# Where the high parts of the weights lie in the second projection

## What is computed

```
p = rmsnorm(x, ln_g[l]) @ w_in[l]          # 1024 -> 3584 columns: the projection
mixer a, b, c = p[:2304] ; xq = next 256 ; gate = last 1024
o = band attention (layer 0) or a gated linear recurrence (layer 1) on a, b, c
y = concat(o, cross_attention(xq, memory)) * silu(gate)
x = x + y @ w_out[l]
```

## The kernel before

| | place before |
|---|---|
| x, high and low parts, 9 slots (`x.slot`) | byte 480 of 512; slots 0 to 6 at 480 of 1024, 7 and 8 at 992 |
| one slice k of x | 1280 bytes in the first pass, 1024 later |
| weights, high part, low part and sum | byte 32 of 512, which `pj1_shift0` and `pj1_shift1` (64 bytes each) give |
| one slice k of the weights | 512 bytes |

## Time and profile before

### The profile page before, as it was taken

One profiled execution on the slowest core, in us unless ns is written; L12 is line 12 of the kernel. 1 busy time (PEld: TensorE's weight loads), 2 busy tenths in 40 slices (PEclk: granted clock), 3 DMA queues, 4 the chain that ended last, 5 costly groups with the idle time before them and its releaser, 6 DMA issues. The chain is left out here.

```text
span 2376.1 us, 61711 instructions
## 1 busy us (share of the span) xinstructions
PE 2312.2 (97%) x23787; PEld 2094.7 (88%) x23787; DVE 1819.5 (77%) x3555; ACT 1413.5 (59%) x3281; POOL 381.0 (16%) x585
## 2 busy tenths in 40 slices
PE   7999999999989999999999999999999989999998
PEld 4999999999967888888887999999999978888886
DVE  7889788887666656666666998797888777888885
ACT  4564666755565555555554564776757566666664
POOL 2332000000022221211112332000000112112111
PEclk9999999999999999999999999999999999999999
DMA  6886887769894222222226897886879793444442
GB/s 227 298 299 219 301 281 231 247 220 332 232 307 121 83 66 89 90 69 83 73 81 232 272 303 242 256 275 214 266 248 312 230 269 117 129 131 122 137 135 70
DMA packets 396664, 469.64 MB, mean 198 GB/s; under 512 B 39860, under 2 KB 248556, under 8 KB 396376
## 3 DMA queue, kind: packets, MB, share of 16 engines
q1 hardware_dynamic: 379832, 406.02, 54.4%
q0 software_dynamic: 14704, 54.92, 6.6%
q10 hardware_dynamic: 1840, 4.75, 0.7%
HBM read 318.77 MB, written 151.56 MB: 198 GB/s over the span
## 5 line engine op out<-in xcount | busy, mean ns | idle before, releaser
L1468 PE MATMUL pj_acc<-x_lo,pj_wh 128*128 128x256 f32 (+1 forms) x3080 | 780.9, 284 | 0.0
L1468 PE MATMUL pj_acc<-x_hi,pj_wh 128*128 128x256 f32 (+1 forms) x3080 | 780.8, 284 | 0.0
L1468 PEld LDWEIGHTS pj_acc<-x_hi,pj_wh 128*128 128x128 f32 x3080 | 578.4, 188 | 0.0
L1468 PEld LDWEIGHTS pj_acc<-x_lo,pj_wh 128*128 128x128 f32 x3080 | 578.4, 188 | 0.0
L509 ACT ACTIVATE pj_wh<-pj_wt 128x512 fp32r<-128x512 f32 x676 | 420.3, 634 | 255.9 <-DMA pj_wt<-tsum 175.1
L516 DVE SCALAR_TENSOR_TENSOR pj_wl<-pj_wt,pj_wh 128x512 fp32r<-128x512 f32 x676 | 467.0, 708 | 87.0 <-ACT pj_wh L509 79.3
L1464 PE MATMUL pj_acc<-x_hi,pj_wl 128*128 128x256 f32 (+1 forms) x3080 | 509.4, 287 | 13.8 <-DVE pj_wl L516 11.9
L1464 PEld LDWEIGHTS pj_acc<-x_hi,pj_wl 128*128 128x128 f32 x3080 | 425.3, 188 | 22.1 <-DVE pj_wl L516 19.5
L1307 DVE TENSOR_TENSOR pj_out<-pj_out,pj_acc 128x512 f32<-128x512 f32 (+1 forms) x448 | 320.8, 716 | 103.3 <-PE pj_acc L1468 69.7
L2541 DVE COPY pb_pt<-pb_SCTP 128x256 f32<-128x256 f32 (+2 forms) x266 | 115.8, 435 | 147.5 <-PE pb_SCTP L2352 74.3
L2676 ACT ACTIVATE pb_se<-pb_se,pb_mn 128x640 f32<-128x640 f32 (+4 forms) x208 | 154.6, 745 | 114.6 <-DVE pb_mn L2524 114.3
(11 more groups left out here) (371 smaller groups left out, 3992.1 us busy)
## 6 DMA issues: line engine op xcount, KB each, us to landing
pj_wt<-tsum SPq DMA_DIRECT2D x546, 256.0 KB, 3.8
proj<-pj_out SPq DMA_DIRECT2D x112, 512.0 KB, 4.2
tsum<-pj_wt SPq DMA_DIRECT2D x140, 256.0 KB, 3.2
pj_wraw<-in_w_in_dram POOLq DMA_DIRECT2D x24, 1024.0 KB, 6.6
tsum<-pj_wraw SPq DMA_DIRECT2D x56, 256.0 KB, 4.2
hg_x<-x_mid SPq DMA_DIRECT2D x17, 512.0 KB, 3.7
pb_gate<-proj SPq DMA_DIRECT2D x16, 512.0 KB, 5.1
pb_x<-in_x_prompt_dram SPq DMA_DIRECT2D x16, 512.0 KB, 3.8
```

Source lines behind the costliest of these rows:

```text
L1468: ins = nc.tensor.matmul(BANK[j][:, 0:n], w.hi[j][:, k], x.of(y, p, j)[:, k], start=False, stop=(k == 3 and i == 1))
```

## The change

In the second projection the high parts get buffers of 4 slices of 136 columns, of which 128 are used, so that slices lie 544 bytes apart. Ahead of term j stands an empty buffer of 128 x (j mod 4) bytes, and behind it one that fills up, so that the low part and the next term begin at byte 32 of a 512-byte period again. The high parts of the terms start at byte 32, 160, 288, 416, 32, 160 and 288 of 512. An empty buffer `pj1_pad1` is shortened so that the x slots behind term 0 stay where they were. The first projection keeps its layout.

```diff
     def term(self, j, sb, shadowed):
         l = self.l
-        self.hi[j] = sb(f"pj{l}_wh{j}", [P, 4, P], F32R)
+        if l:
+            if j % 4:
+                sb(f"pj{l}_apart{j}", [P, j % 4 * 32])
+            self.hi[j] = sb(f"pj{l}_wh{j}", [P, 4, P + 8], F32R)[:, :, 0:P]
+            if j % 4 < 3:
+                sb(f"pj{l}_again{j}", [P, 96 - j % 4 * 32])
+        else:
+            self.hi[j] = sb(f"pj{l}_wh{j}", [P, 4, P], F32R)
         with ExitStack() as shadow:
             self.sum[j] = shadowed(shadow)(f"pj{l}_wt{j}", [P, 4, P])
         self.lo[j] = sb(f"pj{l}_wl{j}", [P, 4, P], F32R)
...
                         w.term(0, sb1, sb_in)
-                        sb1("pj1_pad1", [P, 496])
+                        sb1("pj1_pad1", [P, 368])
                         for i in (1, 2, 0, 4, 5, 6):
```

## The result

| | before | after |
|---|---|---|
| median of the runs, us | 2383.94 (5 runs) | 2395.55 (5 runs) |
| ratio | | 1.0047, 95% interval 1.0035 to 1.0059 |
| span of the profiled execution, us | 2376.1 | 2392.0 |
| first rounded narrow step starts, us | 1473.97 | 1476.68 |
| last narrow step starts, us | 1886.12 | 1901.54 |

The account below looks back on a forecast made before the run. TensorE was taken to bound the second projection through the distance between matmul starts. All terms (high-part matmuls, rounding, subtraction, buffer shift) were 0, leaving the 2384.9 us median, predicted as 2385 us; range 2370 to 2398.

Parts of the forecast that it names:

- the slower rival: Second projection's high-part matmuls: changing distances lose the fast rhythm again and again; +12.7 us, 2397.6 us; chance 0.26.
- sign of being wrong: Second projection's matmul starts: a pattern by slice or term, or TensorE waiting for VectorE in the wide pass.
- What bounds the kernel: Second projection: TensorE, by distance between matmul starts, 113.3 ns in narrow passes and 146.7 ns in the wide one.
- I take 0, for four reasons: Second projection's high-part matmuls: no change, 0 us, between bounds of -24.5 and +12.7 us.
- Reasons two and three: Second projection: no slice dearer in the wide pass despite 256-byte jumps; no x slot much dearer in narrow passes.
- Reason one: Narrow passes: 117.5 and 113.3 ns rhythms have the same address distances, so addresses did not set the rhythm.
- Reason four: Attention stage's output matmuls: buffers differing by 32 bytes gave 0.22 and 0.23 us between starts, under 5%.
- The faster rival: Second projection's high-part matmuls: spread placements avoid part of the read collisions; -12.3 us, 2372.6 us; chance 0.29.
- The 8.8 us around the span: Whole kernel: median 2384.9 us against the profile's 2376.1 us; the difference was taken to lie around the span and left.
- The rounding and subtraction in four runs: Second projection: ScalarE writes and VectorE reads high parts as four runs of 128; 0 us each, subtraction at worst +2.2.

## Why the prediction was right in its range and wrong in its likeliest case

The time, 2395.55 us, lies in the range of 2370 to 2398, near the slower rival's 2397.6. The forecast itself, no change and 2385 us, was wrong: what came true is the rival that had a chance of 0.26. The range held because it had been drawn to reach that rival. The prediction's own sign of being wrong, a pattern by slice or by term in the starts, is there: in the last pass terms 0 to 6 take 1.43, 1.41, 1.42, 1.40, 1.42, 1.42 and 1.42 us a step.

- **What bounds the kernel** was right: TensorE waited even less in the narrow passes, and of the 15.8 us that their matmuls lost from start to start, 12.7 reached the end.
- **The slower rival's total** is near the time partly by luck, since its terms missed both ways. It had 9.9 us for the narrow high-part matmuls, which lost 11.1. It had nothing for the low parts' matmuls, which lost 4.7, since four at the good distance are about what the rhythm takes to come back. The shorter pauses, 3.0 us, stood nowhere in it. And it had 2.8 us for the wide pass, whose matmuls lost nothing.
- **The step that failed is "I take 0, for four reasons".** Reasons two and three looked at distances that jump by 256 and 512 bytes. Both are multiples of 128, and the runs show that just those jumps are free (offsets by term, spacing of 640). Distances of 0, 32 or 96 modulo 128 were nowhere in this stage's trace, and I read their absence as harmlessness. What the runs showed in place of the 0 is 118.4 ns for 113.7 on the matmuls with high parts.
- **Reason one** was true and its conclusion was not. Two rhythms on one layout do exist, but at distance 64 modulo 128 alone; at the others nothing below 116.8 ns lasts. That a state can change by itself doesn't show that the layout has no part in it.
- **Reason four** had the only fine distance in the trace, 32 bytes, in matmuls of 512 columns in groups of three with other instructions between. Their starts lie 226 to 240 ns apart, with medians of 231 to 233 ns on every full tile. And the two distances compared there, 0 and 96 modulo 128, are both such as never had the fast rhythm in the projection, so they could not have shown one being lost.
- **The slower rival's mechanism** was nearly the one at work: a fast rhythm that holds at one distance and is lost at slices. It was argued as a matter of change from slice to slice, and its counter-argument (the wide pass has changing distances and stays regular) rested on the same blind spot. What decides is each distance's remainder, not that it changes: 96 or 128 held constant is as slow.
- **The faster rival** (half the excess goes when meetings are spread) did not occur in any layout tried. The 109.2 ns that the prediction worked out from the Trainium skill was reached in no steady stretch of any layout, and 113.3 was the lowest. The page "TensorE: Matmul & The Clock Gate" of the Trainium skill, section "Back-to-back issue gap", gives that formula for a single matmul by itself and not for a stream with a weight load each, which the prediction didn't say.
- **The 8.8 us around the span** were a misreading: about 1.8 us lie around it in every run of the changed kernel, and the rest, by these figures, was a profiled execution quicker than the median. It did not touch the forecast, which left them as they were.
- The rounding and subtraction in four runs cost nothing, as said.

The prediction set aside a rule of the Trainium skill, page "TensorE: Matmul & The Clock Gate", section "Step-by-step: what each phase is for", that a load of the next weights takes nothing from the running matmul. It would have made this change free. For fp32r streams of 256 columns the runs speak against it: with instructions, counts and sizes equal, a distance of 96 or 128 bytes instead of 64 between the two operands' places costs 5.4 ns a matmul (118.7 against 113.3), and with both operands moved together by 64 bytes 113.3 is still reached. The page "SBUF — State Buffer", section "SBUF: two separate sides", says that TensorE never waits on anyone else's accesses. No run here contradicts that: what was moved are TensorE's own two operands. Why the distance matters, and whether a load meets the stream of its own matmul or of the one before, these runs don't tell.

## What to carry to other kernels

Where matmuls with a weight load each run without a wait, read the distance from start to start and compare it over layouts: one matmul's recorded duration hides it. Here it paid to keep every spacing of slices of either operand at a multiple of 128 bytes, so that the distance between the two has one remainder modulo 128, and to choose the good remainder, 64; for other forms the good one has to be measured. And when a trace is used to call a parameter harmless, check first that the trace holds values of the kind that the change brings in.

## What the hardware showed that was not expected

- The fast rhythm, 113.3 ns a matmul of 256 fp32r columns with its weight load, was seen with weights 64, 192, 320 and 448 bytes past x's place in 512, and in no steady stretch at another distance. The others tried had 116.8 to 120.0 ns. 0 and 96 modulo 128 were also tried as the only distance of a kernel, 32 modulo 128 was not.
- At distance 64 both 113.3 and 117.7 ns are steady. A stretch entered in the slow one can stay there for 16 steps (the starts from 1473.97 to 1495.16 us before) or 47 (the last ones of the kernel with offsets by term). A pause can end it, or the passage through another distance; but the stretch of 47 was begun by a pause.
- In the first projection, whose layout no kernel here changed, between 166 and 255 of the 294 narrow steps were fast, by execution. At 4.4 ns a matmul or 53 ns a step, 89 steps are 4.7 us (an estimate). Runs of the kernel before on one chip spread over up to 12.4 us, so this can be a part of that spread.
- In the wide pass (320 columns) the mean without pauses stayed between 145.8 and 146.9 ns in all layouts; why 64 more columns make it nearly insensitive is open.
